# Gate and up of the layers' feed-forward stages as seven block products instead of eight

## What is computed

```python
def _swiglu(x, w_gate, w_up, w_down):
    return (jax.nn.silu(x @ w_gate) * (x @ w_up)) @ w_down

for l in range(DEPTH):                                   # DEPTH = 2
    x = x + 0.5 * _swiglu(_rms_norm(x, norm_ffn1[l]), ffn1_w_gate[l], ffn1_w_up[l], ffn1_w_down[l])
    ...                                                  # the mixer: rwkv, attention, convolution
    x = x + 0.5 * _swiglu(_rms_norm(x, norm_ffn2[l]), ffn2_w_gate[l], ffn2_w_up[l], ffn2_w_down[l])
```

## Time and profile before

| | |
|---|---|
| median of three runs | 1386.77 us |
| the profiled execution: span | 1389.5 us |
| TensorE busy | 98% of the span |
| VectorE / ScalarE / GpSimd busy | 70% / 53% / 12% |
| mean granted TensorE clock | 0.992 |
| two groups of a feed-forward stage, steady | 33.2 us |

### The profile page before, as it was taken

How to read it: one execution, slowest core, us unless ns; L and a number is a source line. 1 busy time by engine, 2 the same in 40 slices (tenths; PEclk the granted TensorE clock), 3 DMA queues, 4 the chain that set the end, 5 groups by cost and what they waited for, 6 DMA issues and landing times.

```text
span 1389.5 us, 24785 instructions
## 1 busy us (share of the span) xinstructions
PE 1361.1 (98%) x9701; PEld 1181.9 (85%) x9701; DVE 975.5 (70%) x1312; ACT 737.4 (53%) x1050; POOL 162.0 (12%) x158
## 2 busy tenths in 40 slices
PE   9999999999999999999999999999999999999997
PEld 7888889987888888888888987888888998788885
DVE  6666666766776666766666766686666675898887
ACT  6444467464654445644447655464444444755553
POOL 3000000197000000000000059300000033000000
PEclk9999999999999999999999999899999999999999
DMA  9856264113385645755529120466563953456540
GB/s 338 264 194 196 96 199 150 60 65 119 126 262 186 192 138 183 257 189 182 181 67 296 54 92 30 128 202 193 183 198 102 296 191 114 148 194 211 190 142 31
DMA packets 170483, 230.57 MB, mean 166 GB/s; under 512 B 4687, under 2 KB 151815, under 8 KB 170149
## 3 DMA queue, kind: packets, MB, share of 16 engines
q1 hardware_dynamic: 167920, 223.75, 49.2%
q10 hardware_dynamic: 1877, 5.59, 1.0%
q0 software_dynamic: 608, 0.12, 0.1%
HBM read 228.39 MB, written 2.63 MB: 166 GB/s over the span
## 4 chain that ended last, share of the span: by engine, by line
PE 89%; DVE 5%; ACT 3%; issue 1%; POOL 1%; DMA 1%; ACTq 0%; POOLq 0%; SPq 0%; DVEq 0%
PE bank L478 37%; PE bank L646 27%; PE bank L650 14%; PE bank L1502 3%; DVE down_lo L463 1%; ACT down_hi L458 1%; PE bank L601 1%; PE bank L1178 1%; PE bank L1168 1%; PE bank L1369 1%; PE bank L1309 1%; DMA w_gate<-in_ffn_w_gate_dram 1%; DVE up_lo L463 0%; DVE gate_lo L463 0%; PE bank L929 0%
## 5 line engine op out<-in xcount | busy, mean ns | idle before, releaser
L646 PE MATMUL bank<-hT,up_hi 128*128 128x512 f32 x880 | 220.8, 393 | 0.0
L463 DVE TENSOR_TENSOR down_lo<-w_down,down_hi 128x2048 fp32r<-128x2048 f32 (+1 forms) x65 | 147.7, 2273 | 93.5 <-ACT down_hi L458 93.5
L725 ACT ACTIVATE work<-bank 128x256 f32<-128x256 f32 x176 | 66.9, 384 | 258.2 <-PE bank L650 257.9
L646 PE MATMUL bank<-hT,gate_hi 128*128 128x512 f32 x800 | 199.8, 392 | 0.0
L458 ACT ACTIVATE down_hi<-w_down 128x2048 fp32r<-128x2048 f32 (+1 forms) x65 | 123.6, 1902 | 115.9 <-PE bank L478 115.9
L646 PEld LDWEIGHTS bank<-hT,up_hi 128*128 128x128 f32 x880 | 158.2, 189 | 29.2 <-issue 0.6
L463 DVE TENSOR_TENSOR up_lo<-w_up,up_hi 128x2048 fp32r<-128x2048 f32 x72 | 164.2, 2280 | 16.6 <-ACT up_hi L458 16.5
L463 DVE TENSOR_TENSOR gate_lo<-w_gate,gate_hi 128x2048 fp32r<-128x2048 f32 x64 | 146.9, 2296 | 36.7 <-ACT gate_hi L458 36.7
L646 PEld LDWEIGHTS bank<-hT,gate_hi 128*128 128x128 f32 x800 | 146.9, 188 | 28.6 <-DVE gate_lo L463 0.3
L478 PE MATMUL bank<-down_hi,ff_hi 128*128 128x512 f32 x400 | 156.2, 391 | 0.0
L478 PE MATMUL bank<-down_lo,ff_hi 128*128 128x512 f32 x400 | 156.2, 391 | 0.0
(11 more groups left out here) (379 smaller groups left out, 2312.0 us busy)
## 6 DMA issues: line engine op xcount, KB each, us to landing
w_up<-in_ffn_w_up_dram SPq DMA_DIRECT2D x44, 1024.0 KB, 5.4
w_down<-in_ffn_w_down_dram SPq DMA_DIRECT2D x44, 1024.0 KB, 5.2
w_gate<-in_ffn_w_gate_dram SPq DMA_DIRECT2D x43, 1024.0 KB, 5.4
w_up<-in_w_in_dram SPq DMA_DIRECT2D x12, 1024.0 KB, 9.3
w_gate<-in_w_up_dram SPq DMA_DIRECT2D x11, 1024.0 KB, 5.1
w_up<-in_w_up_dram SPq DMA_DIRECT2D x11, 1024.0 KB, 5.1
w_down<-in_w_down_dram SPq DMA_DIRECT2D x11, 1024.0 KB, 4.9
w_down<-in_w_in_dram SPq DMA_DIRECT2D x9, 1024.0 KB, 8.4
```

The costliest lines, as they stand in the source:

```text
L463: dve.tensor_tensor(staged[kind][1][:, 0:cols], slot[sl][:, 0:cols], staged[kind][0][:, 0:cols].bitcast(F32), ALU.subtract).then_inc(split ...
L646: pe.matmul(bank[:, :], w[0][:, c, at], hpair[:, :, c, :], start=c == 0, stop=False)
L725: act.activation(to[:, q, j * SEQ:(j + 1) * SEQ], psum[2 * q + j][:, SEQ:], ACT.Copy)\
```

## The change

One group (256 features) stays as it was. The other ten are taken in five pairs of 512 hidden features, here called steps. For one step the activations are four blocks A[t][k] (t: tokens 0-127 or 128-255; k: first or second half of the 1024 features) and the weights four blocks of 512 x 512: gate and up, each for k = 0 and 1. The result has four blocks too (gate and up, for two t), and Strassen's algorithm gets them from seven block products P1 to P7 instead of eight. Now the activations are the stationary operand (128 x 128) and the weights stream in 512 columns: a block product is 4 x 3 = 12 matmuls of 512 columns.

Three of the products use a weight block as it was loaded (P1: gate, k 0; P2: gate, k 1; P3: up, k 1). The other four use sums of blocks, formed on GpSimd for every step (T1 to T4, each 128 x 2048 floats). T1 goes into the `mix` buffer, the other three overwrite slots. Four sums and differences of activation blocks are formed once in a stage, with four more GpSimd instructions that put hi and lo together.

All seven blocks and the two down tiles of a step are staged by ScalarE and VectorE as before, so nine splits take the place of six. The staged buffers are a ring of three (extra, down, gate) for the blocks and one ("up") for the down tiles. The result now has tokens on the partitions, so the hidden values are turned for the down product: four TensorE transposes of 128 x 128 for each half of the tokens. The loops over groups are unrolled. Other edits rename and merge semaphores of the mixers and move small buffers.

```diff
+P1, P2, P6, P5, P7, P3, P4 = range(7)
+T_SLOTS = ("gate0", "up0", "gate0", "mix", "gate1", "up1", "up0")
+RING = ("extra", "down", "gate")
...
+            def quarter_product(s, i, bank, acts, first):
+                kind, _ = t_use(s, i)
+                ...
+                for c in range(4):
+                    mm = product(pe, psum[bank][:, :], lambda p_: acts[p_][:, c, :], lambda p_: w[p_][:, c, :],
+                                 first and c == 0, c == 3, skip_group_check=True)
+                mm.then_inc(used[kind], 1)
...
+            for s in range(1, SUPER + 1):          # TensorE; SUPER = 5
+                p1(s)
+                if s == 1:
+                    p2(s)
+                    down(0)
+                else:
+                    turn(s - 1, 1)
+                    down(2 * s - 3)
+                    p2(s)
+                p6(s)
+                p5(s)
+                if 1 < s < SUPER:
+                    down(2 * s - 2)
+                p7(s)
+                p3(s)
+                p4(s)
+                turn(s, 0)
+            down(2 * SUPER - 2)
+            turn(SUPER, 1)
+            last_downs()
...
+            for s in range(1, SUPER + 1):          # SyncE
+                if s > 1:
+                    tile(2 * s - 1)
+                sp.wait_ge(S["t_sum"], 4 * s + 20 * f + past["t_sum"])
+                if s < SUPER:
+                    gate(0, s + 1)
+                tile(2 * s)
+                if s < SUPER:
+                    up(0, s + 1)
+                    up(1, s + 1)
+                    gate(1, s + 1)
...
+            def t1(s):                             # GpSimd
+                staged_(3 * s - 3)
+                ...
+                landed("gate0", s)
+                landed("gate1", s - 1)
+                inc(pool.tensor_tensor(T_FROM["mix"], slot["gate0"][:, :], slot["gate1"][:, :], add))
+
+            def others(s):
+                landed("up1", s - 1)
+                staged_(3 * s - 2)
+                sums(4 * s - 3)
+                inc(pool.tensor_tensor(slot["gate0"][:, :], T_FROM["mix"], slot["up1"][:, :], add))
+                inc(pool.tensor_tensor(slot["gate1"][:, :], slot["gate1"][:, :], slot["up1"][:, :], add))
+                staged_(3 * s - 1)
+                sums(4 * s - 2)
+                inc(pool.tensor_tensor(slot["up0"][:, :], slot["gate0"][:, :], slot["up0"][:, :], add))
```

More of the change, by code:

```diff
@@ L42 @@
 OUT_SLOTS = ["gate0", "up0", "down0", "down1"]
-OUT_KINDS = ["down", "up", "gate", "down"]
+OUT_KINDS = ["down", "up", "gate", "extra"]
 OUT_PAIRS = (2, 1, 0, 3)
@@ L287, in build @@
         taps, o = area(o, 2, 2, 512)
-        hN, _ = area(o_ffn, NT, D)
+        hN, _ = area(16384, NT, D)
+        low, _ = area(13312, 2, 512)
+        whole, _ = area(15360, 2, 512)
+        held = [area(16384 + 512 * i, 512)[0] for i in range(3)]
+        diag, o = area(19968, 2 * P)
+        rms_row, o = area(o, 2 * P)
+        ones_now, o = area(o, P)
+        assert o <= WORK
         ld, o = area(12288, 3, SEQ)
@@ L587, in pe_bias_row, with pe_layer_ffn @@
               .then_inc(bias_mm, 1)
-        def pe_ffn(pe, uses, f, n_norm, last="gate", raw=True, front=False, order=HALVES, turns=None, by_half=False):
-            b = f * GROUPS
+        def pe_layer_ffn(pe, uses, f, n_norm, front=False, order=HALVES, turns=None):
             def open_gate(w):
@@ new lines, in pe_layer_ffn, with pe_ffn, open_gate @@
+            down(2 * SUPER - 2)
+            turn(SUPER, 1)
+            last_downs()
+            if turns:
+                turns[1]()
+            uses.layer_ffn()
+        def pe_ffn(pe, uses, n_norm, last="gate"):
+            def open_gate(w):
+                for c in range(KC):
+                    h_ready(pe, n_norm, c)
+                    for j in range(2):
+                        pe.matmul(psum[j][:, :], w[0][:, c, j * P:(j + 1) * P], hpair[:, :, c, :],
+                                  start=c == 0, stop=False)
+                    for j in range(2):
+                        mm = pe.matmul(psum[j][:, 0:SEQ], w[1][:, c, j * P:(j + 1) * P], hT[0][:, c, :],
+                                       start=False, stop=c == KC - 1)
+                        if (c, j) == (KC - 1, 0):
+                            mm.then_inc(S["gu_mm"], 1)
+                mm.then_inc(used["gate"], 1)
@@ L1668, in pe_mix @@
             pe_turn_next(pe, 2, MIX_PLACES)
-            uses.each(OUT_SLOTS)
+            uses.out()
         def act_mix(act, uses):
```

752 lines of the change are left out of this document (532 added, 220 removed).

## The result

The changed kernel takes 1667.71 us, the median of four runs (1666.85 to 1668.72). The kernel before took 1389.15 us in the same comparison (1385.81 to 1393.36). The ratio is 1.2015 with a 95% interval of 1.1981 to 1.205: 20% slower. The forecast was 1530 us with a range of 1450 to 1600. Its direction held, its size did not: 278 us more instead of 141.

A forecast was written before the change was run, and what follows sets the result against it. Bound before by TensorE's matmuls, then by a loop of mutually exclusive GpSimd sums and VectorE splits plus refill: four stages 35 us longer (140), plus 6, take 1389.5 to 1535, less 2.7 to the median: 1530 us, range 1450 to 1600.

The forecast's parts named there:

- TensorE's work, 30.9 us a step: TensorE per step: seven block products 19.1 us, transposes 0.9, two down products 10.9; against 33.2 before, 46 us less in all.
- A free sum, 4.5 us: One unblocked GpSimd weight sum of 128 x 2048 was taken as 4.5 us, four as 18 us a step.
- The rival of cheap sums: GpSimd's weight sums take 3.9 us each, giving 1487 us, or 1445 with packing at the floor; chance 0.22.
- Sum and split exclude each other over 2048 columns: GpSimd sums and VectorE splits block each other whole instructions long; their exclusive time was put at 37.3 us a step.
- The loop, 39.4 us a step: T1 to next T1: sums 18.0, three splits 6.6, work after T4 7.2, gate1's fetch 5.4, one more split 2.2 us.
- the packing: VectorE gets a waiting split in at each of the three changes between GpSimd's four sums, 6.6 us together.
- The first step, T1 of step 2 at 43 us: Start of a stage: activation sums between T1 and T2, T4 ends at 33.2, P7 split at 37.6, next T1 at 43.
- the 217.6 of the prediction: A whole stage: 43, three steps 118.2, last step 39, TensorE alone 17.4 us; 182.7 before, so 35 more.
- The end of a stage, 56.4 us: Last step 39 us from T1, then three down products and two turns on TensorE alone, 17.4 us.
- The clock, 66 us if it fell: Rival: TensorE's waits halve its clock some 7 us a step, 3.3 us each, 66 more, about 1596 us; chance 0.15.
- The first stage, 6 us more than the others: First stage: activation sums ahead of T1, and transfers at 332 GB/s with DMA engines 97% busy; 6 us added.
- Unrolling and semaphores, nothing: Unrolled loops and renamed semaphores were costed at nothing, the sequencers' work lying beside waits; some microseconds if either showed.

The follow-up runs named there:

- short sums: Changed kernel with each of GpSimd's four weight sums of a step covering 64 of 2048 columns, all waits kept: 1433.68 us, one run.
- the filler: Changed kernel with TensorE multiplying a constant, matmuls that nothing reads, where it would wait: 1672.94 us, ratio 1.2064.
- writes only: Changed kernel with each of the four weight sums of a step replaced by three GpSimd memsets, some 4.5 us together: 1467.51 us, one run.
- nothing left: Changed kernel with weight sums over 64 columns, activation sums as memsets, and step 1's up tiles fetched before the second gate tile: 1413.04 us, one run.
- up tiles first: Changed kernel with SyncE fetching step 1's up tiles before the second gate tile in the three stages after the first: 1651.46 us, ratio 1.1891.
- no activation sums: Changed kernel with the eight GpSimd activation sums of a stage replaced by memsets, weight sums kept: 1643.88 us, one run.
- P7 and the refill first: Changed kernel with P7 ahead of the down tile in steps 2 to 4, and gate1's refill ahead of the down tile's fill in steps 2 and 3: 1689.67 us.
- sums on VectorE: Changed kernel with the four weight sums of a step on VectorE ahead of P6's split, activation sums left on GpSimd: 1588.34 us, one run.
- both edits of the first step: Changed kernel with up tiles fetched ahead of the second gate tile and the eight activation sums replaced by memsets: 1635.01 us, one run.

## Why the prediction was wrong, step by step

- *TensorE's work, 30.9 us a step*: too small. Where nothing else holds TensorE up for long, a step is 32.1 us (short sums, three whole steps). Against 33.2 that saves 1.1 us a step, 22 in all, not 46.
- *A free sum, 4.5 us*: right, 4.5 to 4.6. The rival of cheap sums is out.
- *Sum and split exclude each other over 2048 columns*: right. It makes 200 of the 278 us (writes in place of sums).
- *The loop, 39.4 us a step*: 41.4 in stage 3, and 43.3 and 42.6 for the two steps from 112.02 in stage 1. Two terms were too small. The refill of slot gate1 takes 6.1 us in the median (the page's part on DMA issues: count, KB each, median us to landing), 6.3 in the step shown, not the 5.4 of the earlier trace rows. And VectorE does not get a split in at each change: between T2 and T3 nothing of 2048 columns stood ready (the product of 0.6 us got in), so P6's split ran after T4 and made the wait behind T4 15.7 us instead of 12.6. The prediction named the packing as its weakest point, and rightly.

```profile
w_gate<-in_ffn_w_gate_dram SPq DMA_DIRECT2D x23, 1024.0 KB, 5.2
w_gate<-in_ffn_w_up_dram SPq DMA_DIRECT2D x20, 1024.0 KB, 6.1
```

- *The first step, T1 of step 2 at 43 us*: measured 65.2 (65.9 and 64.8 in the second and fourth stage), and this is the step that failed. It is 22.2 of the 38.0 us by which stage 3 exceeds the 217.6 of the prediction. It had the eight activation sums at their free 1.1 to 1.27 us, 9.5 us, though the same text had shown such sums blocked by splits; they take 16.4. And it let T1 start at once, without reading SyncE's queue, where its tile stands behind a tile whose slot is not free: 16.9 us. With both taken away T1 of step 2 comes at 48.9. That these two make the first step late is shown; but together they bring only 33 of the 138 us that the forecast lacks, since the step behind the first gets longer, as told below, and the loop and the end stay as they were.
- *The end of a stage, 56.4 us*: 66.1. The last step needs the same blocked splits: with writes in place of sums, and GpSimd as busy as before, it is 53.1.
- *The clock, 66 us if it fell*: it fell, to 0.90 over stage 3, but the filler took most of it back and gained nothing in all. As a rival with a price of its own it was wrong.
- *The first stage, 6 us more than the others*: it grew least, from 185.9 to 251.9 us. *Unrolling and semaphores, nothing*: the four stages account for all of it, 66.0 + 71.4 + 70.3 + 71.4 = 279.

In stage 3 the 70.3 us part as follows: the mutual blocking 255.6 - 209.7 = 45.9; the length of the weight sums 209.7 - 197.2 = 12.5; activation sums and late up tile 197.2 - 190.3 = 6.9, with the weight sums short; and 5.0 that the new order costs by itself (stage lengths of the changed kernel, writes only, short sums, nothing left, before 185.3). Of the 45.9 us only 5.5 lie in the first step, 27.4 in the three steps behind it and 13.0 in the end. The first step goes from 65.2 to 59.7 us with writes only, then to 49.1 with short sums and to 39.7 with nothing left: there it is mostly the row of operations on GpSimd, one behind the other, and not their blocking by weight sums.

Why a shorter first step gives little away: the average of the steps behind it rises by 1.0 to 1.5 us in three kernels (up tiles first, no activation sums, both), and all of it lies in one step. From T1 of step 2 to T1 of step 3 it is 39.2 us in the changed kernel and 43.6, 43.4 and 43.2 in these three; the two steps behind that take 85.1 together, and 84.0 to 85.6. T2 of step 2, in the changed kernel and with the up tiles first:

```profile
762.52 4.57 POOL L1251 TENSOR_TENSOR w_gate<-mix,w_up 128x2048 f32<-128x2048 f32 x1 [2.29 <-DVE down_lo L1117]
```
```profile
749.47 4.61 POOL L1251 TENSOR_TENSOR w_gate<-mix,w_up 128x2048 f32<-128x2048 f32 x1 [7.29 <-DVE down_lo L1117]
```

In the changed kernel VectorE begins P4's split and a down tile's (751.33 and 753.54) before T1 begins at 754.51. In the three others T1 comes before both, and T2 must wait for both and for P1's split behind them. An earlier T1 runs into VectorE's queue.

What stays open: what the half clock costs by itself, and why the kernel with P7 and the refill first loses 6 us behind T1 of step 4. Short sums, writes only, sums on VectorE, no activation sums, both edits of the first step and nothing left have one run each; the differences that carry the argument, 24 us and more, are beyond the 12 us by which the runs of one kernel here differ at most. The 9 us between both edits of the first step and no activation sums alone are not.

## What to carry to other kernels

A saving on the engine that is 98% busy is worth its face value only while every other engine keeps its slack. Before GpSimd gets work beside VectorE, add up both engines' instructions of the kinds that exclude each other as if one engine did them, and compare this with the time of the step. In a pipeline work out the first step as carefully as the steady one, from the queue's order and the slots, and with blocked durations. And before a step's length is read as an engine's work, count that engine's instructions in the window.

## What the runs showed of the hardware

- A GpSimd memset of 128 x 2048 floats takes 1.81 us, and it neither holds up VectorE's split nor is held up by it. A sum of that size takes 4.5 to 4.6 us free, and a split begun 0.4 to 0.5 us after one takes 6.26 to 6.69.
- The blocking holds for small instructions too: VectorE's product of 512 columns with both inputs in SBUF took 4.54 us beside T1 (706.66), where 0.69 is its free time.
- GpSimd's sum of 64 columns (L1252) took 0.32 us on average with nothing left on GpSimd, 0.39 with short sums, against 4.5 us for 2048.
- Filler matmuls raised the mean granted clock from 0.932 to 0.974, and the time stayed (1667.71 and 1672.94 us).
